# Gate and projection pieces ahead of the turns of probabilities on TensorE, in a decoder layer with two kinds of attention

## The chip, the core and the metric

The kernel runs on one core of one Trainium2 chip. The core has five engines that matter here, each working through its own instructions in order and waiting for the others by semaphores: TensorE (PE; matmuls, and transposes as matmuls with the identity), VectorE (DVE), ScalarE (ACT), GpSimd (POOL) and SyncE (SP, which issues the loads). The metric is the device time in microseconds; the figure for a kernel is the median of its runs.

## The reference

One layer of a decoder, 512 tokens of width 1024, all in 32-bit floats:

```
h = rms_norm(x)
q, k, v | q, kv of three branches | branch gates | merge gates = h @ w_in
y_A = block-sparse attention, 8 heads        y_B = three-branch attention, 8 heads, 2 kv groups
x = x + (sigmoid(gA) * (y_A @ W_A) + sigmoid(gB) * (y_B @ W_B)) @ w_o
x = x + (gelu(conv_a) * conv_b) @ w_down     conv = causal conv3 of rms_norm(x) @ w_up
x = x + sigmoid(x @ w_pg) * (p @ w_pp)
```

Queries and keys are normalised per head; a table of relative positions is added to every logit. With 512 tokens every block that attention may choose is chosen, so each branch is a causal softmax attention; the compressed branch has 31 keys.

## The kernel before, in words

A 32-bit product is made of three products of rounded operands: each factor is split into a high half (a copy rounded to the matmul's format) and a low half (the rest), and `three` (L1489) issues high x high, high x low and low x high. ScalarE or VectorE makes the high half, VectorE or GpSimd the low.

**Units.** The combined projection is cut into units w = 0 to 7, each a set of 256 to 384 columns (`ucols`). `project` (L1511) multiplies one unit with one tile tt of 128 tokens, in 8 pieces kt along the width of 1024; 3 matmuls make a piece. From unit 1 on a unit brings queries and keys for one pair of heads, n = w - 1 (unit 6: queries of two pairs). Its life: the weights are split (`w_high`, `w_low`, `split_unit`); TensorE projects; ScalarE copies the result out of its PSUM bank (`take_proj`, L838) and squares it; VectorE sums and makes a first guess of the root, GpSimd refines it in 12 small operations (`root`), VectorE normalises the tile (`normalise`, L1257); TensorE turns it (`turn_tile`, L1551) into PSUM bank 1; ScalarE and VectorE take high and low half out of it (`tile_high` L875, `tile_low` L1276). There is one such bank, so each tile waits for the low half of the one before.

**Gates.** The merge gates are 16 products of 128 columns by 512 tokens (`gate`, L1554), in 8 pieces kt of 3 matmuls, all into bank 7. ScalarE takes a gate by a tanh (`take_gate`, L918). For units 3 to 5 bank 7 is a projection bank too, for tiles 1 and 3 (`proj_bank`).

**Attention steps.** The work of attention is a list of 100 steps: 8 for each of the pairs 0 to 3, 17 for each of the pairs 4 to 7 (two branches, and one compressed step that ends the pair). A step t is one head's scores for one tile of queries, i + 1 blocks of 128 keys wide, i = 0 to 3 in turn. Each engine runs a loop over t. On TensorE step t has, before the change: the scores of t; the turn of the probabilities of t - 3 (`turn_probs`, L1650: `LAG` is 3); if due, a product with the values (`values`, L1672, 5 steps late); then pieces of a gate or of a projection that the tables `GATE` and `PROJ` give to this step; then the turn of a normalised tile if the table `TURN` says so. In a pair's first step the scores come behind the projection pieces, since they may need them. On ScalarE (L988 to L1016) the order in a step is:

```
take_gate, take_proj + squares (of what ended in step t-1); take_probs(t-3); tile_high(TURN[t-1]);
exp(t); gate_high; gather_strip; w_high(SPLIT[t])
```

VectorE has `bias(t)` (adds the position table and finds the maximum), `invert(t-1)`, the sums, `tile_low(TURN[t-1])`, `w_low(SPLIT[t])`, `normalise(TILE[t])` and the guess. GpSimd has `scale(t-1)`, its part of the splits, and `root`. The tables are filled by rules of step numbers (L119 to L150); no planner with costs is in it. Four banks of PSUM hold scores and turned probabilities, two each, so that step t's instructions wait for those of t - 2.

Of the kernel before, what the change touches and what calls it, by code (L numbers as in the profile page):

```python
# [73 lines left out]
def layer(nc, A, out):  # L74
    STEPS = attention_steps()
# [20 lines left out]
    GATE, j = {}, 2  # L96
# [24 lines left out]
    for w in range(2, W_UNITS):  # L121
        b0 = first_t[w - 2]
        if w == 2:
            start, counts, row = b0, (4, 4), ROWS - KT
        elif w < 6:
            start, counts, row = b0 - 4, (5, 6, 5, 5, 6, 5), 0
        elif w == 6:
            start, counts, row = b0 - 4, (4,) * 8, 0
        else:
            start, counts, row = b0 - 6, (2,) * 16, 0  # L130
        for a, count in enumerate(counts):
            PROJ[start + a] = (w, row, row + count)
            row += count
        split0 = b0 - 8 if w == 7 else b0 - 7
        for a in range(KT // 2):
            SPLIT[split0 + a] = (w, range(2 * a, 2 * a + 2))
        VALUES[start + len(counts)] = w
        ends = [t for t in sorted(PROJ) if PROJ[t][0] == w for r in range(*PROJ[t][1:]) if r % KT == KT - 1]
        for half in range(2):
            t = ends[2 * half + 1] + 1 if w > 2 else b0 + 2 * half  # L140
            GUESS[t] = (w, half)
            late = 1 if half and w < 6 else 0
            if late:
                ROOT[t + 1], ROOT[t + 2] = (w, half, range(1)), (w, half, range(1, 3))
            else:
                ROOT[t + 1] = (w, half, range(3))
            if w >= 6:
                late += 1
            for a in range(2):
                TILE[t + 2 + late + 2 * a], TURN[t + 3 + late + 2 * a] = (w, 2 * half + a), (w, 2 * half + a)  # L150

    def segments(t):

# [13 lines left out]
    LAG = 3  # L167
    VLAG = LAG + 2
# [43 lines left out]
    with ExitStack() as ctx:  # L212
# [123 lines left out]
        qkv_done = sem("qkv_done")  # L336
# [62 lines left out]
        def proj_bank(w, tt):  # L399

            if w == 0:
                return (0, 1, 4, 5)[tt]
            if w in (3, 4, 5):
                return 7 * (tt % 2)
            return 6 if w <= 2 and tt % 2 and (w, tt) != (2, 3) else 0

        def column(w, x):
# [1080 lines left out]
        def _(pe):  # L1488
# [22 lines left out]
            def project(w, tt, kts=range(KT)):  # L1511

                c = ucols(w)
                if kts[0] == 0:
                    before = 4 * w + tt - (1 if w > 5 or (w, tt) in ((2, 3), (3, 0)) else 2)
                    if before >= 0:
                        pe.wait_ge(qkv_done, before + 1)
                    if w in (3, 4, 5) and tt == 1:
                        pe.wait_ge(gate_tanh, w)
                for kt in kts:  # L1520
                    wait_weights(pe, w, kt)
                    pe.wait_ge(hT_lo, kt + 1)
                    t_ = slice(P * tt, P * (tt + 1))
                    ins = three(PS[:, proj_bank(w, tt), 0:c], hTh[:, kt, t_], hTl[:, kt, t_], Wh[:, kt, 0:c], Wl[:, kt, 0:c], kt == 0, kt == KT - 1)
                    if tt == NT - 1 and kt < KT - 1:
                        ins.then_inc(w_used, 1)
                if kts[-1] == KT - 1:
                    ins.then_inc(proj_filled, 1)
# [25 lines left out]
            def gate(j, kts=range(KT)):  # L1554

                if kts[0] == 0:
                    pe.wait_ge(g_lo[0], j + 1)
                    if j:
                        pe.wait_ge(gate_tanh, j)
                    if j == 2:  # L1560
                        pe.wait_ge(vc_done, 1)
                    if j in (3, 4, 5):
                        pe.wait_ge(qkv_done, 4 * j + 4)
                for kt in kts:
                    if kt == 4:
                        pe.wait_ge(g_lo[1], j + 1)
                    ins = three(PS[:, 7, :], Gh[j % 2][:, kt, :], Gl[j % 2][:, kt, :], hTh[:, kt, :], hTl[:, kt, :], kt == 0, kt == KT - 1)
                if kts[-1] == KT - 1:
                    ins.then_inc(gate_filled, 1)
# [152 lines left out]
            for t in range(T):  # L1722
                if STEPS[t]["k"]:
                    scores(t)
                if t >= LAG:
                    turn_probs(t - LAG)
                if t >= VLAG and STEPS[t - VLAG]["due"]:
                    values(t - VLAG)
                opens = t in PROJ and PROJ[t][1] % KT == 0
                if t in GATE and opens:  # L1730
                    gate(*GATE[t])
                if t in PROJ:
                    for part in segments(t):
                        project(*part)
                if not STEPS[t]["k"]:
                    scores(t)
                if t in GATE and not opens:
                    gate(*GATE[t])
                if t in TURN:
                    turn_tile(*TURN[t])  # L1740

# [186 lines left out]
```

## Time and profile before

| | |
|---|---|
| median of 3 runs | 888.48 us (887.63 to 891.33) |
| the profiled execution | 890.37 us, span 888.5 us |
| TensorE busy | 863.6 us, 97% |
| VectorE, ScalarE, GpSimd busy | 378.0, 405.8, 425.3 us (43, 46, 48%) |
| chain that ended last | 88% on TensorE |
| attention steps on TensorE | from about 82 to 372 us of the span |

A row of the timeline gives start, length, engine, line, operation, operands, the count of instructions merged in it and, in brackets, how long the engine had been idle before and who ended that. TensorE's matmuls are pipelined: the start of the next instruction, not the row's length, tells what one costs. Steps are found in the timeline by the scores: those of step 18 start at 151.63 us, those of step 30 at 197.65 us, those of step 38 at 220.01 us, those of step 93 at 351.01 us.

### The profile page before, as it was taken

To read this page: it belongs to the slowest core of one execution; us is meant where nothing else is said; L and a number is where in the kernel's file an instruction comes from. 1 tells how busy PE (TensorE), PEld (TensorE's weight loads), DVE (VectorE), ACT (ScalarE), POOL (GpSimd) and SP (SyncE) were. 2 spreads that over 40 slices of the span, in tenths; PEclk is the share of its full clock that TensorE was granted. 3 is DMA by queue.
4 is the path that set the end of the run, shared out by engine and by line. 5 is a ranking of instruction groups with operands and counts; after the bars stand their busy time and mean duration, and the time that the engine had idled before them with its cause. 6 is when DMAs were issued, how large, how long until landed. Compare 5 with 4: busy or idle time off the path is not lost.

```text
span 888.5 us, 13023 instructions
## 1 busy us (share of the span) xinstructions
PE 863.6 (97%) x4471; PEld 726.9 (82%) x4471; DVE 378.0 (43%) x864; ACT 405.8 (46%) x882; POOL 425.3 (48%) x547
## 2 busy tenths in 40 slices
PE   8999999999799999999999999999999999999998
PEld 8899889887688776788887888888888888888886
DVE  5446665555545534444417444444444440020223
ACT  5224656566646667533433744444444442231321
POOL 3841764554534345644552644444444444454440
PEclk9999999999999999999999999999999999999999
DMA  6944443342121226266531633333333333332214
GB/s 188 232 109 131 107 103 95 96 113 60 37 60 50 70 85 214 81 233 211 187 95 56 206 94 95 95 98 101 99 97 106 99 98 98 97 102 86 83 62 140
DMA packets 101363, 99.30 MB, mean 112 GB/s; under 512 B 15956, under 2 KB 76084, under 8 KB 101300
## 3 DMA queue, kind: packets, MB, share of 16 engines
q1 hardware_dynamic: 101247, 98.48, 37.7%
q8 instruction: 37, 0.61, 0.3%
q14 instruction: 26, 0.21, 0.1%
q10 hardware_dynamic: 53, 0.01, 0.0%
HBM read 87.58 MB, written 10.88 MB: 111 GB/s over the span
## 4 chain that ended last, share of the span: by engine, by line
PE 88%; DVE 4%; ACT 3%; issue 2%; POOL 2%; SPq 0%; DMA 0%; ACTq 0%; DVEq 0%; POOLq 0%
PE banks L1491 26%; PE banks L1492 25%; PE banks L1493 25%; PE banks L1672 3%; PE banks L1650 2%; PE banks L1630 1%; PE banks L1629 1%; PE banks L1551 1%; PE banks L1680 1%; ACT attention_split L875 1%; DVE plain_arena L1290 1%; DMA plain_arena<-in_conv_w_dram 0%; DVE plain_arena L1257 0%; PE banks L1579 0%; PE banks L1508 0%
## 5 line engine op out<-in xcount | busy, mean ns | idle before, releaser
L698 POOL TENSOR_TENSOR split_arena<-plain_arena,split_arena 128x512 fp32r<-128x512 f32 x184 | 240.2, 1318 | 252.0 <-ACT split_arena L932 232.5
L1491 PE MATMUL banks<-split_arena 128*128 128x512 f32 (+3 forms) x808 | 304.2, 376 | 5.3 <-ACT plain_arena L838 2.1
L1493 PE MATMUL banks<-split_arena 128*128 128x512 f32 (+3 forms) x808 | 296.8, 367 | 0.0
L1492 PE MATMUL banks<-split_arena 128*128 128x512 f32 (+3 forms) x808 | 296.7, 367 | 0.0
L932 ACT ACTIVATE split_arena<-plain_arena 128x512 fp32r<-128x512 f32 x184 | 112.9, 627 | 190.0 <-PE banks L1493 175.2
L1491 PEld LDWEIGHTS banks<-split_arena 128*128 128x128 f32 x808 | 152.4, 189 | 31.9 <-issue 3.5
L1493 PEld LDWEIGHTS banks<-split_arena 128*128 128x128 f32 x808 | 152.0, 188 | 21.1
L1492 PEld LDWEIGHTS banks<-split_arena 128*128 128x128 f32 x808 | 152.4, 189 | 20.3 <-issue 0.5
L1491 PE MATMUL banks<-late_arena,split_arena 128*128 128x512 f32 x240 | 93.8, 391 | 0.0
L1493 PE MATMUL banks<-late_arena,split_arena 128*128 128x512 f32 x240 | 93.5, 390 | 0.0
L1492 PE MATMUL banks<-late_arena,split_arena 128*128 128x512 f32 x240 | 93.5, 389 | 0.0
L1449 DVE SCALAR_TENSOR_TENSOR plain_arena<-banks,plain_arena 128x511 f32<-128x511 f32 x44 | 32.7, 743 | 133.2 <-ACT plain_arena L1041 133.2
L1290 DVE CUSTOM_DVE_ANT_0 plain_arena<-banks,plain_arena 128x128 f32<-128x128 f32 (+1 forms) x96 | 46.8, 487 | 74.0 <-PE banks L1630 73.8
L886 ACT ACTIVATE plain_arena<-plain_arena 128x128 f32<-128x128 f32 (+1 forms) x96 | 53.9, 562 | 37.7 <-DVE plain_arena L1290 37.5
L713 POOL TENSOR_SCALAR plain_arena<-plain_arena 128x128 f32<-128x128 f32 (+1 forms) x64 | 40.0, 627 | 61.3 <-DVE plain_arena L1308 61.1
L911 ACT ACTIVATE attention_plain<-banks 128x128 f32<-128x128 f32 (+1 forms) x96 | 41.3, 430 | 57.9 <-PE banks L1650 57.4
L1493 PEld LDWEIGHTS banks<-late_arena,split_arena 128*128 128x128 f32 x240 | 45.1, 188 | 9.5
L1491 PEld LDWEIGHTS banks<-late_arena,split_arena 128*128 128x128 f32 x240 | 45.1, 188 | 9.2
L1492 PEld LDWEIGHTS banks<-late_arena,split_arena 128*128 128x128 f32 x240 | 45.1, 188 | 9.2
L1650 PE MATMUL banks<-plain_arena 128*128 128x128 f32 x240 | 42.5, 277 | 1.7 <-POOL plain_arena L713 1.7
L1467 DVE TENSOR_TENSOR plain_arena<-banks,plain_arena 128x512 f32<-128x512 f32 x8 | 5.0, 683 | 86.5 <-PE banks L1493 86.5
L1041 ACT ACTIVATE plain_arena<-banks,plain_arena 128x512 f32<-128x512 f32 x44 | 30.6, 777 | 22.3 <-PE banks L1493 22.3
(193 smaller groups left out, 1113.4 us busy)
## 6 DMA issues: line engine op xcount, KB each, us to landing
plain_arena<-in_w_up_dram SPq DMA_DIRECT2D x88, 256.0 KB, 3.2
plain_arena<-in_w_down_dram SPq DMA_DIRECT2D x44, 256.0 KB, 2.6
plain_arena<-in_w_in_dram SPq DMA_DIRECT2D x18, 512.0 KB, 4.2
plain_arena<-in_w_in_dram SPq DMA_DIRECT2D x32, 192.0 KB, 4.0
plain_arena<-in_x_dram SPq DMA_DIRECT2D x8, 512.0 KB, 5.0
gates<-plain_arena SPq DMA_DIRECT2D x16, 256.0 KB, 2.4
plain_arena<-skew SPq DMA_DIRECT2D x16, 256.0 KB, 4.6
plain_arena<-gates SPq DMA_DIRECT2D x16, 256.0 KB, 3.6
```

Source lines behind the costliest of these rows:

```text
L698: pool.tensor_tensor(W2l[:, c % RING, :], raw2[:, c % RING, :], W2h[:, c % RING, :].bitcast(F32), ALU.subtract).then_inc(w2_lo, 1)
L713: pool.tensor_scalar(p_, p_, r, gsig[:, s["i"], h:h + 1], ALU.mult, ALU.mult).then_inc(scaled, 1)
L886: nc.scalar.activation(prob[:, t % 4, 0:nk], prob[:, t % 4, 0:nk], ACT.Exp, bias=mneg[:, t % 4:t % 4 + 1], scale=-1.0, accum_out=rsum[:, t ...
L911: nc.scalar.activation(PT[:, u % 4, 0:i + 1, P * i:P * (i + 1)], PS[:, 4 + t % 2, 0:P * (i + 1)].rearrange("p (j q) -> p j q", j=i + 1), A ...
L932: nc.scalar.activation(W2h[:, c % RING, :], raw2[:, c % RING, :], ACT.Copy).then_inc(w2_hi, 1)
L1041: nc.scalar.activation(dst[:, f % 2, :], PS[:, b, :], ACT.Identity, scale=cst[:, CONVW + 88 + col:CONVW + 89 + col], bias=cst[:, CONVB + c ...
L1290: nc.vector.tensor_tensor_reduce(out=prob[:, t % 4, 0:nk], in0=PS[:, 2 + t % 2, 0:nk], in1=strip[:, n % 2, e, S - nk:S], scale=1.0, scalar ...
L1449: link(nc.vector.scalar_tensor_tensor(out=dst[:, f % 2, 1:S], in0=PS[:, b, 0:S - 1], scalar=cst[:, CONVW + 44 + col:CONVW + 45 + col], in1 ...
L1491: nc.tensor.matmul(o, ah, bh, start=first, stop=False)
L1492: nc.tensor.matmul(o, ah, bl, start=False, stop=False)
L1493: return nc.tensor.matmul(o, al, bh, start=False, stop=last)
L1650: ins = nc.tensor.transpose(PS[:, 4 + t % 2, P * j:P * (j + 1)], prob[:, t % 4, P * j:P * (j + 1)], ident)
```

## The change

On TensorE, `turn_probs` and `values` move behind the gate and projection pieces of their step. Three tables change with it: the weights of unit 3 are split one step earlier (`split0`); the tiles of unit 6 are normalised three steps apart in place of two and turned two steps after; those of unit 7 are turned two steps after they are normalised. Unit 6 gets bank 7 for its tile 1, and the waits for projection banks are set accordingly.

```
-        split0 = b0 - 8 if w == 7 else b0 - 7
+        split0 = b0 - 8 if w in (3, 7) else b0 - 7
...
+            gap, lead = (3 if w == 6 else 2), (2 if w >= 6 else 1)
             for a in range(2):
-                TILE[t + 2 + late + 2 * a], TURN[t + 3 + late + 2 * a] = (w, 2 * half + a), (w, 2 * half + a)
+                TILE[t + 2 + late + gap * a], TURN[t + 2 + late + gap * a + lead] = (w, 2 * half + a), (w, 2 * half + a)
...
+            if w == 6:
+                return 7 * (tt == 1)
...
-                    before = 4 * w + tt - (1 if w > 5 or (w, tt) in ((2, 3), (3, 0)) else 2)
+                    before = 4 * w + tt - (1 if w > 6 or (w, tt) in ((2, 3), (3, 0), (6, 0), (6, 3)) else 2)
...
-                    if w in (3, 4, 5) and tt == 1:
+                    if w in (3, 4, 5, 6) and tt == 1:
...
+                    if j == 6:
+                        pe.wait_ge(qkv_done, 4 * 6 + 2)
...
                 if STEPS[t]["k"]:
                     scores(t)
-                if t >= LAG:
-                    turn_probs(t - LAG)
-                if t >= VLAG and STEPS[t - VLAG]["due"]:
-                    values(t - VLAG)
                 opens = t in PROJ and PROJ[t][1] % KT == 0
...
                 if t in GATE and not opens:
                     gate(*GATE[t])
+                if t >= LAG:
+                    turn_probs(t - LAG)
+                if t >= VLAG and STEPS[t - VLAG]["due"]:
+                    values(t - VLAG)
                 if t in TURN:
                     turn_tile(*TURN[t])
```

TensorE at the border of steps 17 and 18, before: the last matmuls of the projection of unit 4 (128x384), the scores of step 18, the turn of the probabilities of step 15 (4 blocks), and the first matmuls of gate 4 (128x512).

```order
L1491 MATMUL banks<-split_arena 128x384
L1492 MATMUL banks<-split_arena 128x384
L1493 MATMUL banks<-split_arena 128x384
L1629 MATMUL banks<-attention_split 128x384
L1630 MATMUL banks<-attention_split 128x384
L1650 MATMUL banks<-plain_arena 128x128 x4
L1491 MATMUL banks<-split_arena 128x512
L1492 MATMUL banks<-split_arena 128x512
```

The same place with the change; the lines have moved by 3 to 5 (L1655 is the turn, L1634 and L1635 the scores).

```order
L1494 MATMUL banks<-split_arena 128x384
L1495 MATMUL banks<-split_arena 128x384
L1496 MATMUL banks<-split_arena 128x384
L1655 MATMUL banks<-plain_arena 128x128 x3
L1634 MATMUL banks<-attention_split 128x384
L1635 MATMUL banks<-attention_split 128x384
L1494 MATMUL banks<-split_arena 128x512
L1495 MATMUL banks<-split_arena 128x512
```

The turn of step 14 (3 blocks), which stood ahead of the projection, now follows it, and the gate follows the scores of step 18 at once. ScalarE around the same border has the same operations in both: copy of the probabilities of step 14, two copies of a tile, the exponential, two weight conversions, and the projection tile's copy, on which the gate depends.

```order
L914 ACTIVATE attention_plain<-banks 128x3x128
L878 ACTIVATE attention_split<-banks,plain_arena 128x2x128 x2
L889 ACTIVATE plain_arena<-plain_arena 128x256
L846 ACTIVATE split_arena<-plain_arena 128x384 x2
L841 ACTIVATE plain_arena<-banks 128x384
```

These are rows with the change; before they read L911, L875, L886, L843 and L838 in the same order. Only the moment at which the first can start has moved.

TensorE in steps 40 and 41, before: scores (128x128), turn of 2 blocks, tile 2 of unit 6 (L1551), scores (128x256), turn of 3 blocks, gate 7.

```order
L1629 MATMUL banks<-attention_split 128x128
L1630 MATMUL banks<-attention_split 128x128
L1650 MATMUL banks<-plain_arena 128x128 x2
L1551 MATMUL banks<-plain_arena 128x128 x4
L1629 MATMUL banks<-attention_split 128x256
L1630 MATMUL banks<-attention_split 128x256
L1650 MATMUL banks<-plain_arena 128x128 x3
L1491 MATMUL banks<-split_arena,attention_split 128x512
```

The same steps with the change (L1554 is the turn of a tile).

```order
L1634 MATMUL banks<-attention_split 128x128
L1635 MATMUL banks<-attention_split 128x128
L1655 MATMUL banks<-plain_arena 128x128 x2
L1554 MATMUL banks<-plain_arena 128x128 x4
L1634 MATMUL banks<-attention_split 128x256
L1635 MATMUL banks<-attention_split 128x256
L1494 MATMUL banks<-split_arena,attention_split 128x512
L1495 MATMUL banks<-split_arena,attention_split 128x512
L1496 MATMUL banks<-split_arena,attention_split 128x512
L1655 MATMUL banks<-plain_arena 128x128 x3
L1554 MATMUL banks<-plain_arena 128x128 x4
```

Tile 1 is turned in step 40 now and tile 2 in step 41, right behind the turn of the probabilities of step 38.

## Rows read from the trace of the kernel before

**Rows 1.** The page: TensorE's busy share, and its granted clock in 40 slices.

```profile
PE 863.6 (97%) x4471; PEld 726.9 (82%) x4471; DVE 378.0 (43%) x864; ACT 405.8 (46%) x882; POOL 425.3 (48%) x547
...
PEclk9999999999999999999999999999999999999999
```

**Rows 2.** Waits of TensorE, 88 to 380 us: in total, times, longest.

```profile
PE banks L1551 <- DVE plain_arena L1257: 5.6, 4, 2.6
PE banks L1491 <- ACT plain_arena L838: 2.6, 3, 1.3
PE banks L1491 <- DVE split_arena L1173: 1.9, 2, 1.2
PE banks L1650 <- POOL plain_arena L713: 1.7, 3, 0.9
PE banks L1647 <- DVE plain_arena L1316: 1.3, 2, 0.8
```

**Rows 3.** Timeline of TensorE, two of these waits: start, length, operation.

```profile
204.21 0.39 PE L1491 MATMUL banks<-split_arena 128*128 128x256 f32 x1 [1.25 <-ACT plain_arena L838]
...
233.00 0.63 PE L1551 MATMUL banks<-plain_arena 128*128 128x128 f32 x4 [2.58 <-DVE plain_arena L1257]
```

**Rows 4.** Timeline of ScalarE in steps 17 and 18.

```profile
149.76 0.47 ACT L911 ACTIVATE attention_plain<-banks 128x384 f32<-128x384 f32 x1
150.13 0.83 ACT L875 ACTIVATE attention_split<-banks,plain_arena 128x256 fp32r<-128x256 f32 x2
150.84 0.52 ACT L886 ACTIVATE plain_arena<-plain_arena 128x256 f32<-128x256 f32 x1
...
151.33 0.94 ACT L843 ACTIVATE split_arena<-plain_arena 128x384 fp32r<-128x384 f32 x2
152.16 0.49 ACT L838 ACTIVATE plain_arena<-banks 128x384 f32<-128x384 f32 x1
```

**Rows 5.** Timeline of TensorE in the same steps.

```profile
148.69 0.49 PE L1650 MATMUL banks<-plain_arena 128*128 128x128 f32 x3
...
151.63 0.33 PE L1629 MATMUL banks<-attention_split 128*128 128x384 f32 x1
...
151.98 0.60 PE L1650 MATMUL banks<-plain_arena 128*128 128x128 f32 x4
152.80 0.47 PE L1491 MATMUL banks<-split_arena 128*128 128x512 f32 x1 [0.22 <-ACT plain_arena L838]
```

**Rows 6.** Timeline, steps 29 and 30: from a turn of probabilities to a normalised tile.

```profile
195.89 0.49 PE L1650 MATMUL banks<-plain_arena 128*128 128x128 f32 x3
...
196.42 0.49 ACT L911 ACTIVATE attention_plain<-banks 128x384 f32<-128x384 f32 x1 [3.50 <-PE banks L1650]
...
198.00 0.60 PE L1650 MATMUL banks<-plain_arena 128*128 128x128 f32 x4
...
198.85 0.68 DVE L1257 TENSOR_TENSOR plain_arena<-plain_arena 128x512 f32<-128x512 f32 x1
```

**Rows 7.** Timeline, step 37: from a turn of probabilities to a tile's low half.

```profile
218.98 0.49 PE L1650 MATMUL banks<-plain_arena 128*128 128x128 f32 x3
...
220.76 0.89 DVE L1276 SCALAR_TENSOR_TENSOR attention_split<-banks,plain_arena,attention_split 64x256 fp32r<-64x256 f32 x2 [1.07 <-ACT attention_split L875]
```

**Rows 8.** Timeline of ScalarE in steps 92 and 93.

```profile
349.82 0.49 ACT L911 ACTIVATE attention_plain<-banks 128x384 f32<-128x384 f32 x1 [0.43 <-PE banks L1650]
...
351.22 0.59 ACT L918 ACTIVATE plain_arena<-banks 128x512 f32<-128x512 f32 x1
```

**Rows 9.** Timeline of TensorE at the end of the attention steps.

```profile
362.05 0.27 PE L1650 MATMUL banks<-plain_arena 128*128 128x128 f32 x1
...
365.78 0.50 PE L1491 MATMUL banks<-split_arena 128*128 128x512 f32 x1 [0.66 <-POOL split_arena L771]
```

**Rows 10.** Stretches: length, busy time and count by engine, granted clock, DMA share, GB/s.

```profile
200.00:230.00 30.00, 26.37 (x182) 22.41 (x181) 17.78 (x64) 19.98 (x59) 14.97 (x37) 1.00 0.18 54
...
233.00:237.00 4.00, 4.00 (x14) 3.41 (x15) 2.67 (x9) 3.51 (x11) 2.20 (x3) 0.57 0.21 63
```

## The prediction

> **What bounds the kernel now.** I read the page first: TensorE is busy 97% of the span and its granted clock is 9 tenths or more in every slice [rows 1]. So the order of its work can bring no more than its waits, and it can cost whatever new waits it makes. The second view is the list of TensorE's waits over 88 to 380 us, the stretch with the attention steps [rows 2]. Five kinds matter: turning a normalised tile waits for VectorE's normalisation (5.6 us in 4), a gate or projection waits for ScalarE to empty a projection bank (2.6 in 3), a projection waits for split weights (1.9 in 2), a turn of probabilities waits for GpSimd's scaling (1.7 in 3) or, after a compressed step, for VectorE (1.3 in 2). Together 13.1 us: the most that a better order can win in waits. The third view is the timeline of all engines at single steps, to see what stands in front of the releaser on its own engine.
>
> **What the change moves.** The matmuls stay the same in number and size. In each step TensorE turned the probabilities of three steps before right after the scores; now it does so after the gate and projection pieces. ScalarE's order hardly changes. In its step t it empties a finished projection bank, squares it, copies the turned probabilities of t-3, copies the high half of a tile turned in step t-1, does the exponentials of t, and converts weights. It is in order, so everything behind the copy of probabilities now begins only when TensorE is through with the step's long pieces.
>
> **What goes.** (a) The split of unit 3 comes a step earlier: 1.9 us go. (b) Unit 6 alternates its banks and its tiles are turned a step later, so the wait at 204.21 (1.25 us) and the four tile waits (5.6) go, in the form in which they stand here [rows 2, 3]. (c) The turns after a compressed step get a gate piece as cover: 1.3 go. Of the 1.7 behind GpSimd the two small ones go (0.8); the largest, 0.9, sits behind twelve root operations that start later too, and I keep it. With the rest of the 2.6 (two gate waits, 1.4, counted again below at their new size) that is 12.2 us gone.
>
> **What comes, first term: the gates of pairs 1 to 3.** Step 18 is the pattern. Gate 4 shares bank 7 with projection tile 3 of unit 4, which ends in step 17. Before, TensorE turned the probabilities of step 14 at 148.69, ahead of that projection [rows 5]; ScalarE copied them at 149.76, then did the tile (150.13), the exponential (150.84) and two weight conversions (151.33), and took the projection at 152.16 [rows 4]. That is 2.40 us of ScalarE work, all of it under the projection; the gate began at 152.80, 0.22 us late [rows 5]. Now the turn comes after the projection. From the start of a turn of three blocks to its copy are 0.53 us when ScalarE is free (195.89 to 196.42 [rows 6]); then the same 2.40, the bank copy 0.49 and 0.15 to the gate's start: 3.57. TensorE has between them only the turn and the next scores, 0.34 + 0.35 = 0.69 (151.63 to 151.98 is such a score; the turn is 0.25 to the next start, and 0.09 longer for what follows it). So it waits 3.57 - 0.69 = 2.9 us. Step 10 is the same; in step 26 the weights are 256 wide and the wait is 2.7. Sum 8.5 us. Bounds: 0 if ScalarE's work were still covered, 8.5 as worked out; nothing that I see covers it, since TensorE and ScalarE both run in order, and I take 8.5.
>
> **Second term: tiles of unit 5 and the last tile of unit 6.** From a turn of probabilities to the end of the normalisation of the next tile but one are 3.64 us (195.89 to 198.85 + 0.68 [rows 6]), because bank 1 and VectorE's queue hold it behind the previous tile. This chain starts at the end of step 29 now. TensorE has the turn, the scores and twelve narrow matmuls, 2.11 us (195.89 to 198.00 [rows 6]), and another turn of four, 0.44, then wants the tile: 1.1 us late, and in step 32, by a shorter chain in a shorter step, the same. Tile 3 of unit 6 waits for tile 2's bank in step 34 by the sum of the first term: 2.8 less 1.45 of cover, 1.3. Sum 3.5 us; bounds 0 and 3.5; I take 3.5.
>
> **Third term: tiles 1 and 2 of unit 6.** The new table turns them in steps 40 and 41, one behind the other. Tile 2 needs bank 1, so VectorE's low half of tile 1, which follows ScalarE's high half, which stands behind the copy of the probabilities of step 38; and these are turned immediately before tile 2. From turn to end of low half are 2.67 us (218.98 to 220.76 + 0.89 [rows 7]); with 0.34 for the turn itself and 0.1 to start, TensorE waits 2.4 us. This wait is structural. I take it in full.
>
> **Smaller ones.** At the start of step 95 gate 15 waits for ScalarE to take gate 14. Before, a value product of 2.4 us stood ahead of the gate and covered that. Now the gate goes first: from the turn at the end of step 92, 0.53 + 1.99 (349.82 to 351.22 + 0.59 [rows 8]) + 0.15 = 2.7 against 1.9 of cover (three turns and three scores, estimated from the lengths in [rows 5, 6]): 0.8. The like at steps 66, 78 and 83, and the scores of step 69, make 1.3. Weight pieces of units 4, 5 and 7, converted behind the late copy, come 0.7, 0.7 and 1.1 late; two bank waits of unit 7 add 0.9, gate 7 and the tile at step 40 add 1.7. Sum 7.2 us. Each rests on three or four durations in a row, and a TensorE held up earlier gives the others time; bounds 0 and 7.2, I take half, 3.6. At the end of the attention ScalarE's last exponential (turn at 362.05 [rows 9]) moves back by a gate piece of 1.45 us, and with it the copies that release GpSimd's low half (L771), for which the matmul at 365.78 waits: 1.0 us, bounds 0 and 1.5.
>
> **The clock.** In 233 to 237 us the granted clock is 0.57 on average, that is 1.2 GHz for most of it, right behind the 2.58 us wait at 233.00 [rows 3, 10]; 4.0 x 0.43 = 1.7 us of full-speed work are lost. In 200 to 230 us, with the wait of 1.25 us at 204.21, it was 2.4 GHz throughout. The new waits of 2.9, 2.9, 2.7 and 2.4 lie at the size that cost a fall once. I take two falls against the one here: +1.7 us; bounds -1.7 (none) and +5.1 (four). The Trainium skill, "TensorE: Matmul & The Clock Gate", section "Why this matters for your kernels", says that idle gaps between bursts of matmuls bring the clock back to half. [...]
>
> **The sum.** -12.2 + 8.5 + 3.5 + 2.4 + 3.6 + 1.0 = +6.8, and 1.7 for the clock: +8.5 us. The profiled execution took 890.37 us (span 888.5), 1.9 above the median of 888.48; I put the difference on the median: 897.0 us. With all smaller waits and four falls it is 888.5 + 10.4 + 5.1 = 904.0. With only the first and third terms, no new fall and all that goes gone, it is 888.5 - 12.2 + 8.5 + 2.4 - 1.7 = 885.5.
>
> **Rivals.**
> Rival 1, faster: the projection banks are emptied in time. ScalarE idles under the projection now, and if it reached the bank copy within the 0.69 us that TensorE has, the first term would be nothing and the removed waits would be the result: with the third term, half of the second and no fall, 888.5 - 12.2 + 2.4 + 1.8 - 1.7 = 878.8. It decides from 0.69 us of ScalarE work behind the turn; rows 4 show 2.40. For it speaks that in steps with little work ScalarE is idle for 3 us and more (3.50 at 196.42 [rows 6]). 6%.
> Rival 2, no change: only the structural waits come, the others are taken up by slack that the earlier ones make; between the 885.5 above and one with half the second term and one fall, 889: 888. 18%.
> Rival 3, the clock decides: all four long waits drop it, and the smaller waits come in full: 904. Slower than the forecast, same sign. 20%.
> The forecast itself, new ScalarE waits larger than what goes, 892.5 to 901: 56%.
>
> **How the numbers follow.** A change of 0.5% is 4.4 us, about what a measurement of this kernel can tell from none. Faster by more is rival 1: 0.06. Within it is rival 2 with a little of the forecast's lower edge: 0.20. Slower: 0.74. The range leaves out rival 1, the lower half of rival 2 and the top of rival 3: 888 to 904; the forecast's own range is 892.5 to 901.
>
> **What would show it.** TensorE's list of waits should have a line of some 8.5 us in three for a gate's first matmul behind ScalarE's bank copy (L838 here), each near 2.9, at steps 10, 18 and 26. A tile turn behind VectorE's low half (L1276 here), near 2.4, should stand once, two scores after the one at step 40. The split-weight waits near 98 and 101 us should be gone, and the waits behind the compressed steps too. ScalarE should sit idle under each long projection and be busy behind it. The prediction fails if those three gate waits are under 1 us each, or if their sum is right and the time is still below 889: then slack elsewhere gave it back, and the list of waits will lack the rest of my terms. After each wait of over 2 us the granted clock of the next 4 us tells the last term.

## The result, and the profile after

The changed kernel takes **913.50 us** (median of 3 runs, 912.53 to 915.76) against 888.48: a ratio of 1.0281, 95% interval 1.0259 to 1.0303. It is 25 us slower. The direction was forecast, the size was not: the median lies 16.5 us above the 897.0 that I predicted and 9.5 us above the end of my range.

The profiled execution took 913.5 us, its span is 911.6, so 23.1 us more than the span before. The page after, to be held against [rows 1]:

```profile
PE 870.5 (95%) x4471; PEld 731.3 (80%) x4471; DVE 377.1 (41%) x864; ACT 404.7 (44%) x882; POOL 425.7 (47%) x547
...
PEclk9999999999999999999999999999999999999999
```

The counts of instructions are what they were, and VectorE, ScalarE and GpSimd are busy as long as before, within 1.1 us; TensorE is busy 6.9 us longer, most of it from a slower clock (below), while its share fell from 97 to 95%. The clock line hides what happened to the clock: each fall, a stretch of a few microseconds at 1.2 GHz, is much shorter than a slice. The largest of TensorE's waits after, 60 to 420 us, are these (total, times, longest). Over this stretch all of its waits sum to 30.4 us, and before to 15.3; the lines that answer are in [rows 2], which cover 88 to 380 us, with line numbers lower by 3 to 5.

```profile
PE banks L1494 <- ACT plain_arena L841: 11.0, 7, 2.7
PE banks L1554 <- DVE attention_split L1279: 5.6, 4, 2.4
PE banks L1554 <- DVE plain_arena L1260: 4.6, 4, 1.7
PE banks L1655 <- POOL plain_arena L716: 2.4, 1, 2.4
PE banks L1494 <- ACT plain_arena L921: 1.9, 3, 0.9
PE banks L1494 <- POOL split_arena L774: 1.5, 1, 1.5
```

The first line is what the first term is about. The second, a tile's turn behind VectorE's low half, does not stand in [rows 2] at all. The gate of step 18, on ScalarE and TensorE, answers to [rows 4, 5]:

```profile
157.39 0.49 PE L1655 MATMUL banks<-plain_arena 128*128 128x128 f32 x3
...
157.91 0.49 ACT L914 ACTIVATE attention_plain<-banks 128x384 f32<-128x384 f32 x1 [2.01 <-PE banks L1655]
158.30 0.83 ACT L878 ACTIVATE attention_split<-banks,plain_arena 128x256 fp32r<-128x256 f32 x2
159.01 0.52 ACT L889 ACTIVATE plain_arena<-plain_arena 128x256 f32<-128x256 f32 x1
...
159.50 0.94 ACT L846 ACTIVATE split_arena<-plain_arena 128x384 fp32r<-128x384 f32 x2
160.33 0.49 ACT L841 ACTIVATE plain_arena<-banks 128x384 f32<-128x384 f32 x1
...
160.96 0.47 PE L1494 MATMUL banks<-split_arena 128*128 128x512 f32 x1 [2.73 <-ACT plain_arena L841]
```

From the turn (157.39) to the gate (160.96) are 3.57 us, exactly the sum of the first term: ScalarE is idle for 2.01 us under the projection, then does in a row what it did under the projection before, and TensorE stands still for 2.73 us. The clock, in stretches of 4 us right behind five long waits (length, busy time and count by engine, granted clock, DMA share, GB/s), answers to [rows 10]:

```profile
126.10:130.00 3.90, 3.90 (x21) 3.33 (x22) 2.07 (x5) 0.73 (x2) 1.13 (x2) 1.00 0.93 221
...
161.00:165.00 4.00, 4.00 (x22) 3.43 (x23) 1.09 (x5) 0.86 (x3) 1.56 (x2) 1.00 0.26 66
...
195.60:199.60 4.00, 4.00 (x12) 3.15 (x13) 1.73 (x5) 0.30 (x1) 0.79 (x2) 0.63 0.42 86
...
247.10:251.10 4.00, 4.00 (x16) 3.43 (x17) 1.20 (x4) 1.15 (x3) 1.70 (x3) 0.60 0.50 131
...
309.80:313.80 4.00, 4.00 (x15) 3.38 (x16) 1.36 (x4) 1.21 (x4) 1.91 (x3) 0.63 0.00 0
```

The two longest waits (2.73 us at 126.07 and 160.96) left the clock at 2.4 GHz; those of 2.52, 2.32 and 2.41 us dropped it to 1.2 GHz for some 3.4 us, 1.7 us of work each, and so did one of 1.54 us at 387.96. Four falls against one before are three more: 5.1 us.

The account of the span: waits 15.1, clock 5.1, and 1.7 by which the attention steps began later in this execution. I don't count that start as an effect of the change: the first wait of the stretch, at 84.87 us here and 83.17 before, lies anywhere from 81.6 to 84.5 us in the profiled executions of the ten variants below. Together 21.9 of 23.1 us; 1.2 are not assigned.

### The profile page after: what moved, and what is told of

It reads as the page before. It is cut to its first block, busy times and chain, and to the rows that moved or that the text cites. A ratio compares the mean times of both kernels' runs of the same rounds, so it can differ in the third digit from the quotient of the medians.

```text
span 911.6 us, 13024 instructions
## 1 busy us (share of the span) xinstructions
PE 870.5 (95%) x4471; PEld 731.3 (80%) x4471; DVE 377.1 (41%) x864; ACT 404.7 (44%) x882; POOL 425.7 (47%) x547
## 4 chain that ended last, share of the span: by engine, by line
PE 85%; ACT 4%; DVE 4%; issue 3%; POOL 2%; DMA 1%; SPq 1%; ACTq 0%; DVEq 0%; POOLq 0%
PE banks L1494 25%; PE banks L1496 24%; PE banks L1495 24%; PE banks L1677 3%; PE banks L1655 2%; PE banks L1634 1%; ACT attention_split L878 1%; PE banks L1635 1%; PE banks L1554 1%; ACT plain_arena L889 1%; ACT split_arena L846 1%; POOL split_arena L686 1%; DVE attention_split L1279 1%; PE banks L1685 1%; DMA plain_arena<-in_conv_w_dram 1%
## 5 line engine op out<-in xcount | busy, mean ns | idle before, releaser
L686 POOL TENSOR_TENSOR split_arena<-plain_arena,split_arena 128x384 fp32r<-128x384 f32 (+1 forms) x28 | 31.2, 1117 | 42.2 <-ACT split_arena L846 32.2
L1655 PE MATMUL banks<-plain_arena 128*128 128x128 f32 x240 | 43.1, 279 | 2.5 <-POOL plain_arena L716 2.4
L1279 DVE SCALAR_TENSOR_TENSOR attention_split<-banks,plain_arena,attention_split 64x256 fp32r<-64x256 f32 (+2 forms) x56 | 24.1, 448 | 43.0 <-ACT attention_split L878 42.6
```

Of the source, the lines that this page charges most:

```text
L686: pool.tensor_tensor(Wl[:, kt, 0:c], raw[:, kt, 0:c], Wh[:, kt, 0:c].bitcast(F32), ALU.subtract).then_inc(w_lo[1], 1)
L1279: ins = nc.vector.scalar_tensor_tensor(out=dst, in0=PS[r0:P, 1, P * v0:P * v1].rearrange("p (v c) -> p v c", v=v1 - v0), scalar=cst[r0:P, ...
L1655: ins = nc.tensor.transpose(PS[:, 4 + t % 2, P * j:P * (j + 1)], prob[:, t % 4, P * j:P * (j + 1)], ident)
```

## Experiments

Ratios are against the kernel before on the same chip, in brackets the 95% interval.

**1. The move alone.** The kernel before with its own tables; only `turn_probs` and `values` stand behind the pieces, as in the change:

```
-                if t >= LAG:
-                    turn_probs(t - LAG)
-                if t >= VLAG and STEPS[t - VLAG]["due"]:
-                    values(t - VLAG)
...
                 if t in GATE and not opens:
                     gate(*GATE[t])
+                if t >= LAG:
+                    turn_probs(t - LAG)
+                if t >= VLAG and STEPS[t - VLAG]["due"]:
+                    values(t - VLAG)
```

> The kernel before with one part of the change alone: the turns of probabilities and the value products behind the gate and projection pieces; tables, banks and waits of before. Theory (the loss comes from the move, by way of ScalarE's in-order queue; the tables win back some of it): the three gate waits of 2.5 to 2.7 us and the tile waits for bank 1 are there, and the waits that the tables take away (splits, unit 6) are there too, so 916 to 926 us, slower than the whole change. Rival (the new tables, with tiles turned in neighbouring steps, are the loss): 888 to 896 us.

Measured 919.78 us, 1.0331 (1.0289 to 1.0372). The profiled execution, the slowest of four, has seven falls of the clock. Its largest waits in 60 to 420 us:

```profile
PE banks L1491 <- ACT plain_arena L838: 15.2, 9, 2.7
PE banks L1551 <- DVE plain_arena L1257: 10.2, 5, 2.6
PE banks L1491 <- DVE split_arena L1173: 3.8, 4, 1.9
PE banks L1551 <- DVE attention_split L1276: 2.4, 1, 2.4
```

The move alone makes the whole of the loss. With the tables beside it the time is 4.4 us less by the ratios (0.0050 x 888.5). The uncertainty of that difference is about 4 us by the two intervals, so it is likely, and no more, that the tables give back a part of the loss.

**2. The tables alone.** The changed kernel with the two calls back right behind the scores.

> The change without the move: probabilities are turned right after the scores, as before, with the new tables, banks and waits. Theory: the removed waits of before are pure gain: 1.9 (splits) + 1.3 (bank of unit 6) + some 5 of the tile waits + 1.7 for the fall of the clock behind the longest of them, 9.9 us, so 877 to 882 us. Rival (the tables are the loss): 900 us or more.

Measured 891.30 us, 1.0029 (1.0013 to 1.0045): the forecast of 877 to 882 was wrong. Its largest waits in 60 to 420 us:

```profile
PE banks L1554 <- DVE attention_split L1279: 4.6, 3, 2.6
PE banks L1655 <- POOL plain_arena L716: 3.9, 4, 2.5
PE banks L1554 <- DVE plain_arena L1260: 2.8, 3, 1.8
```

The waits of (a) and (b) are gone from their places; of (c) one of 0.8 us stays (at 336.52), since without the move no gate piece covers it. As many new ones stand there: all waits of the stretch sum to 15.3 us, as before. The large ones are at 95.38 (1.84 us, tile of step 3), at 108.17 (1.23 us), at 229.10 (tile 2 of unit 6, step 41) and at 289.30 (2.46 us, a turn behind GpSimd's scaling). The mean granted clock of the ten executions is 0.995 in the median, against 0.998 for the kernel before on the same chip; that is 2.7 us, as much as the time measured. Steps 40 and 41 show the pattern (timeline):

```profile
225.92 1.05 ACT L926 ACTIVATE split_arena<-plain_arena 128x1024 fp32r<-128x1024 f32 x1
...
226.87 0.48 ACT L914 ACTIVATE attention_plain<-banks 128x384 f32<-128x384 f32 x1
227.24 0.84 ACT L878 ACTIVATE attention_split<-banks,plain_arena 128x256 fp32r<-128x256 f32 x2
...
228.15 0.90 DVE L1279 SCALAR_TENSOR_TENSOR attention_split<-banks,plain_arena,attention_split 64x256 fp32r<-64x256 f32 x2
...
229.10 1.12 PE L1554 MATMUL banks<-plain_arena 128*128 128x128 f32 x4 [2.56 <-DVE attention_split L1279]
```

It is the wait of my third term, without the move (2.56 us here, with the clock at 0.50 in the 4 us behind it): two tiles turned one step apart through one bank. What holds ScalarE up in front of the halves is another thing here, a gate's conversion of 1.05 us (L926) where the changed kernel has the late turn. So the neighbouring turns of the tables are enough for this wait, and the move is not needed for it.

**3. Probabilities early in the three gate steps.** The changed kernel; only in steps 9, 17 and 25 the turn stands ahead of the projection again.

```
+                early = t in (9, 17, 25)
+                if early:
+                    turn_probs(t - LAG)
                 opens = t in PROJ and PROJ[t][1] % KT == 0
...
-                if t >= LAG:
+                if t >= LAG and not early:
                     turn_probs(t - LAG)
```

> The changed kernel, but in steps 9, 17 and 25 alone (the projection that ends a unit's last tile, ahead of a gate in the same bank) the probabilities are turned before the projection, as in before. Theory: the three gate waits (2.73, 2.73, 2.52 us) fall to the size of before (1.2 and 0.2 and none), -6.6 us, and one fall of the clock less, -1.7: 904 to 908 us. Rival (a shorter wait here comes back at the next tile or bank wait): 910 us or more, with the tile waits longer by as much.

Measured 904.81 us, 1.0185 (1.0157 to 1.0213): 8.5 us less by the ratios (0.0096 x 888.5). The line of bank copies falls from 11.0 to 5.6 us; the gates of steps 10, 18 and 26 still wait, 1.56, 0.62 and 0.40 us. So 5.4 of the first term's 8.0 us of waits are shown to hang on the turn ahead of the projection; 6.6 were expected. The other 3.1 us of the 8.5 are no more than the uncertainty of the difference (about 3 us by the two intervals). The rival is out: all other waits of TensorE behind 100 us and up to 400 us are the same as in the changed kernel, to within 0.05 us. One fall of the clock fewer was expected as well; the profile has four again, two of them at other waits than in the changed kernel.

**4. ScalarE's copy last in its step.** The changed kernel with TensorE's order untouched.

```
-                if LAG <= t:
-                    take_probs(t - LAG)
                 if t - 1 in TURN:
                     tile_high(*TURN[t - 1])
...
                 if t in EARLY:
                     split_chunk(EARLY[t])
+                if LAG <= t:
+                    take_probs(t - LAG)
```

> The changed kernel with ScalarE's order in a step altered: the copy of the turned probabilities comes last, behind the tile's high half, the exponential and the weight conversions. TensorE's order is that of the change. Theory (ScalarE's copy of probabilities holds up all that stands behind it): the gate waits fall from 2.7 to about 1 us each, the tile waits for VectorE's low half (5.6 us) to under 1, and two or three falls of the clock go: 892 to 900 us. Rival (TensorE's own order is at fault, through the later scaling and values): 909 us or more.

Measured 884.43 us, 0.9949 (0.9937 to 0.9962): 29 us less than the changed kernel and 4.5 less than the one before, 8 us under the range that I expected. In 60 to 420 us the waits sum to 14.3 us in place of 30.4 (the three gates 1.62, 0.71 and 0.70; tiles behind the low half 3.5 in place of 5.6, where I expected under 1), the profile has no fall of the clock there in place of four (6.8 us), and the attention steps begin 3.0 us earlier, at 81.86. These make 25.9 of the 29.1 us between the two spans; 3.2 are not assigned. The same step as above, in this kernel:

```profile
149.75 0.82 ACT L878 ACTIVATE attention_split<-banks,plain_arena 128x256 fp32r<-128x256 f32 x2
150.47 0.51 ACT L889 ACTIVATE plain_arena<-plain_arena 128x256 f32<-128x256 f32 x1
150.96 0.93 ACT L846 ACTIVATE split_arena<-plain_arena 128x384 fp32r<-128x384 f32 x2
151.79 0.48 ACT L914 ACTIVATE attention_plain<-banks 128x384 f32<-128x384 f32 x1
152.16 0.49 ACT L841 ACTIVATE plain_arena<-banks 128x384 f32<-128x384 f32 x1
```

Halves, exponential and conversions lie under the projection; only the copy and the bank copy follow the turn (151.24), and the gate waits 0.71 us (152.79) in place of 2.73. This shows the cause: with the turn as late as in the changed kernel, the loss is gone once ScalarE, which works in order, no longer holds the rest of the step behind the copy of that turn.

**5. Tile 2 of unit 6 a step later.**

```
+                apart = 1 if (w, half, a) == (6, 1, 0) else 0
-                TILE[t + 2 + late + gap * a], TURN[t + 2 + late + gap * a + lead] = (w, 2 * half + a), (w, 2 * half + a)
+                TILE[t + 2 + late + gap * a], TURN[t + 2 + late + gap * a + lead + apart] = (w, 2 * half + a), (w, 2 * half + a)
```

> The changed kernel with one entry of the table other: tile 2 of unit 6 is turned in step 42, not in 41, so that a step lies between it and tile 1. Theory (TensorE waits for bank 1 because the two turns are neighbours and ScalarE's high half stands behind the late copy of probabilities): the wait of 2.3 us goes, and with it the fall of the clock that began 0.8 us into the next matmuls, 1.7 us: 909 to 911.5 us. Rival (the wait moves to the next tile or scores): 913 us or more.

Measured 908.71 us, 1.0226 (1.0202 to 1.0249), 4.9 us less. The wait at tile 2 shrinks from 2.32 to 0.84 us; I had expected it to go.

```profile
245.43 0.66 PE L1555 MATMUL banks<-plain_arena 128*128 128x128 f32 x4 [0.84 <-DVE attention_split L1280]
```

That is 1.5 us. The profile has one fall of the clock in place of four, but it is the fastest of four executions (906.66 us, mean granted clock 0.998; the others 0.992, 0.991 and 0.989, the changed kernel 0.990, 0.990 and 0.984). By the medians the clock gives 1.4 us. The other 2 us lie within the uncertainty of the difference (about 3 us).

**6. Idle time filled with matmuls.** The changed kernel with 10, 8 and 8 extra matmuls, whose results nobody reads, in the waits of steps 26, 41 and 63. They can't shorten what TensorE waits for; they only keep it at work.

```
+            def fill(t, count):
+
+                pe.wait_ge(biased, t)
+                for _ in range(count):
+                    nc.tensor.matmul(PS[:, 3 - t % 2, :], hTh[:, 0, 0:P], hTh[:, 0, :], start=True, stop=True)
...
+                if t == 26:
+                    fill(t, 10)
...
+                if t == 63:
+                    fill(t, 8)
...
+                if t == 41:
+                    fill(t, 8)
```

> The changed kernel with matmuls that compute nothing put into three of its long waits, in a bank of scores that is free there: 10 ahead of gate 5 in step 26, 8 ahead of the tile in step 41, 8 ahead of the turn of probabilities in step 63 (each 0.23 us; the waits there are 2.5, 2.3 and 2.4 us). The waits last as long as before. Theory (each fall of the clock behind such a wait costs 1.7 us of its own): two or three of the falls go and the time drops by 3.4 to 5.1 us, 908.5 to 910.5 us. Rival (the falls are bookkeeping, or hidden behind other waits): 913 us or more, by what the filler overhangs.

Measured 908.06 us, 1.0223 (1.0202 to 1.0243): 5.2 us less than the changed kernel by the ratios, with 26 matmuls more. From the scores of step 26 to the gate are 3.12 us in both kernels (192.47 to 195.59 in the changed one, 193.69 to 196.81 here), so the work on the way to the gate is as long as it was. Behind it the clock is now full, where it was at 0.63:

```profile
196.80:200.80 4.00, 3.98 (x22) 3.39 (x23) 1.75 (x5) 0.82 (x3) 0.81 (x2) 1.00 0.47 86
```

In 306 to 314 us it is full too; two falls stand in this profile at other places (161.7 and 243.6). The second of them lies over step 41: its eight extra matmuls take 3.21 us, where the eight of step 63 take 1.98, and they overhang the wait. From the start of gate 7 to tile 2 are 4.54 us (243.09 to 247.63) in place of 3.57. The profile is the slowest of the four executions. Over all of them the mean granted clock is 0.9955 in the median against 0.990: 5.0 us less lost to the clock, which is the 5.2 us measured and the price of three falls. The uncertainty of the 5.2 is about 3 us.

**7. ScalarE copies a step later.** The aim is that of experiment 4, but the copies of t - 4 come right behind `take_proj`, so that none of them waits for TensorE in its own step; ScalarE's loop makes one pass more.

```
-                if LAG <= t:
-                    take_probs(t - LAG)
+                if LAG < t:
+                    take_probs(t - LAG - 1)
```

> The changed kernel with ScalarE's copy of turned probabilities a step later in its program: in step t, right after the projection's copy, it copies those of t-4, which TensorE turned at the end of step t-1; then tile, exponential and weights as before. Theory: nothing on ScalarE waits for the end of TensorE's step any more; the gate waits fall from 2.7 to some 0.2 us (with the copy last in its step they kept 0.7 to 1.6), so 880 to 884 us. Rival (with the copy so late, TensorE waits for the banks of turned probabilities or the value products): 888 us or more.

Measured 883.78 us, 0.9946 (0.9925 to 0.9967), not to be told from experiment 4 (0.9949). Its largest waits in 60 to 420 us:

```profile
PE banks L1494 <- ACT plain_arena L841: 2.8, 4, 1.3
PE banks L1554 <- DVE attention_split L1279: 2.3, 2, 1.5
```

11.0 us of bank waits have become 2.8 (the gates of steps 10 and 18 wait 1.28 and 0.33 us, that of step 26 not at all), and a new kind appears, turns that wait for the bank which the late copy holds (1.7 us in two). That is the wait of the rival, too small here to decide the time.

**8. Experiments 7 and 5 together.**

> The lagged copy of probabilities and the tile of step 41 moved to 42 together. Theory: beside the lagged copy alone, the tile wait of 1.5 us that was left at step 41 goes too: 1 to 2 us under it, 879 to 883 us. Rival: with the queue of ScalarE in order the place of that tile costs nothing more, and both are within 0.5 us of each other.

Measured 882.78 us, 0.9931 (0.9911 to 0.9952), the lowest median of all, though 7 and 8 can't be told apart. The tile wait of 1.52 us (at 227.08 in experiment 7) is gone, and one of 0.67 us for split weights stands 6 us further on.

**9. Control: ScalarE's order in the kernel before.** The edit of experiment 4 on the kernel before.

> The kernel before, with TensorE's order and tables untouched; only ScalarE's copy of the turned probabilities stands last in its step, as in the run that won with the move. Theory (ScalarE's order pays only because the move puts the turn behind the long pieces, where the copy blocks tile halves, the exponential, conversions and the bank copy): here the turn comes right behind the scores, ScalarE gets it early, and the copy last delays only the value products, which have two steps of slack: 888 to 892 us, ratio 1.000 to 1.004, and TensorE's waits for the bank copy (L838) stay at 2 to 3 us in sum. Rival (the copy's place was a fault of the kernel before by itself, and the move's win is due to that alone): 882 to 886 us, as with both.

Measured 890.05 us, 1.0010 (0.9998 to 1.0023). Its largest wait in 60 to 420 us:

```profile
PE banks L1650 <- ACT attention_plain L911: 5.2, 7, 1.7
```

These are turns that wait for the late copy, 5.2 us that the kernel before does not have. In return the tile waits behind VectorE's normalisation fall from 5.6 to 1.5 us. The copy's place brings nothing in sum where the turn comes early, but by an exchange of waits and not, as I had expected, because nothing hangs on it. That the late turn is what makes the late copy pay is not shown by itself: experiment 4 has the new tables too, and the tables with the late copy but without the move were not run.

**10. The split of unit 3 back.** The kernel of experiment 8 with the first line of the change undone.

```
-        split0 = b0 - 8 if w in (3, 7) else b0 - 7
+        split0 = b0 - 8 if w == 7 else b0 - 7
```

> The changed kernel with ScalarE's copies of probabilities one step later and tile 2 of unit 6 turned one step later (0.9931 of the kernel before), now with the weights of unit 3 split at their old step. Theory (the earlier split puts a low half on GpSimd, which itself waits 1.00 us for its high half and takes 1.02 us, ahead of the 12 root operations of tile 2 of unit 2, and so causes the 1.7 us wait of a tile turn in step 3): that wait goes, the two waits for split weights near 98 and 101 us (1.9 us) come back, and the time is the same within 1 us: 882 to 884 us, ratio 0.993 to 0.995. Rival (the wait in step 3 belongs to the moved turn): it stays, the split waits come back too: 884.5 to 886 us.

Measured 883.97 us, 0.9940 (0.9922 to 0.9957). Waits in 88 to 104 us, first of experiment 8, then of this one:

```profile
PE banks L1555 <- DVE plain_arena L1261: 1.7, 1, 1.7
```

```profile
PE banks L1495 <- DVE split_arena L1177: 2.2, 2, 1.3
```

One is exchanged for the other. GpSimd shows why (timeline of the changed kernel):

```profile
92.34 1.02 POOL L686 TENSOR_TENSOR split_arena<-plain_arena,split_arena 128x384 fp32r<-128x384 f32 x1 [1.00 <-ACT split_arena L846]
93.32 0.20 POOL L726 TENSOR_TENSOR plain_arena<-plain_arena 128x8 f32<-128x8 f32 x1
...
97.03 0.69 DVE L1260 TENSOR_TENSOR plain_arena<-plain_arena 128x512 f32<-128x512 f32 x1 [2.34 <-POOL plain_arena L732]
...
97.87 0.63 PE L1554 MATMUL banks<-plain_arena 128*128 128x128 f32 x4 [1.72 <-DVE plain_arena L1260]
```

The earlier split stands ahead of the 12 root operations on GpSimd, waits 1.00 us for its high half and takes 1.02; the tile that needs the root comes 1.72 us late.

## Why the prediction was right in direction and wrong in size

**The step that failed: three sizes in the sum.** The mechanism of the loss, ScalarE held up by the late turn, was forecast and is there. The sum put nothing on waits at four places that then measured 6.3 us; it halved the smaller waits (3.6 taken, 6.9 measured); and it took two falls of the clock where the profile has four (1.7 taken, 5.1 measured). The first is the largest.

**What goes (12.2 us): right on its face, wrong as a gain.** The waits that I listed in (a), (b) and (c) are gone. But I priced the tables by the waits they remove and looked for new ones mainly behind the move. Experiment 2 measured the tables by themselves: +0.3%, with as much waiting as before, where I expected 7 to 12 us less. Of the new waits there my sum had only the third term. For (a), "1.9 us go" had a price of 1.72 us on another engine (experiment 10).

**First term (8.5 us): right.** 2.73 + 2.73 + 2.52 = 8.0 us, predicted 2.9, 2.9, 2.7. Each is some 0.2 under what I worked out. Experiment 4 shows the cause (1.62, 0.71 and 0.70 us left), experiment 3 most of the size. Rival 1, which needed ScalarE at the bank copy in 0.69 us, is out: the first long work behind the turn is still the 2.40 us of [rows 4]. But its mechanism is what experiment 4 builds, and the time is then 884, where the rival had 878.8.

**Second term (3.5 us): right.** 1.09 (215.32), 1.24 (221.03) and 1.17 (226.58): 3.5 us.

**Third term (2.4 us): right in size**, 2.32 at 247.08. The table makes it without the move (experiment 2). The old table with the move is no better there: the tiles of unit 6 then wait 1.58, 2.42 and 2.64 us (experiment 1).

**Smaller ones: worked out rightly, then halved on a weak ground.** At the places that I named and right beside them are 6.9 us of waits (split weights 0.48, 0.47 and 0.68; gate 7 and its tile 0.92 and 0.55; seven others of 0.20 to 0.90, 3.8 in all), against 7.2 worked out and 3.6 taken. The ground for halving, that a TensorE held up earlier gives the others time, did not hold: in experiment 3 the gates wait 5.4 us less, and the later waits are the same to within 0.05 us, so they do not depend on how long TensorE was held up before. That fits with ScalarE's work hanging on TensorE's turn, which each wait moves back as well. That is 3.3 us of the miss.

**End of the attention (1.0 us): right**, 1.54 us (at 387.96) in place of the 0.66 of [rows 9]: +0.9.

**Missed: 6.3 us.** The tile of step 3 (1.72); the second tile of unit 2 at 111.94 (2.44); the turn of step 63 behind GpSimd's scaling (2.41, where I had kept 0.9); and 0.58 at 211.06. The second and the last stand in experiment 1 too (2.44 and 0.58), so the move makes them; the other two come with the tables. The second is the chain of the first and third terms at a place where I had not drawn it, from the turn through copy and halves to the freed bank:

```profile
108.90 0.60 PE L1655 MATMUL banks<-plain_arena 128*128 128x128 f32 x4
109.54 0.60 ACT L914 ACTIVATE attention_plain<-banks 128x512 f32<-128x512 f32 x1 [1.09 <-PE banks L1655]
110.03 0.83 ACT L878 ACTIVATE attention_split<-banks,plain_arena 128x256 fp32r<-128x256 f32 x2
...
110.89 0.99 DVE L1279 SCALAR_TENSOR_TENSOR attention_split<-banks,plain_arena,attention_split 64x256 fp32r<-64x256 f32 x2 [1.30 <-ACT attention_split L878]
...
111.94 0.66 PE L1554 MATMUL banks<-plain_arena 128*128 128x128 f32 x4 [2.44 <-DVE attention_split L1279]
```

The third stands in experiment 2 too (2.46), so it comes with the tables. GpSimd's row is the same in the kernel before: a scaling of 128x384, 12 root operations, and the scaling that TensorE waits for. What is new is that a tile of unit 7, turned a step later, has its low half on VectorE (first row, experiment 2) ahead of the reciprocal that the first of these scalings waits for. So GpSimd begins that one 0.81 us later (second row, experiment 2; third row, before), and all that follows it too, while TensorE comes to these steps 0.76 us earlier (a score of 128x384 at 286.50 in place of 287.26). That makes the 1.57 us from 0.89 to 2.46.

```profile
281.60 1.12 DVE L1279 SCALAR_TENSOR_TENSOR attention_split<-banks,plain_arena,attention_split 64x256 fp32r<-64x256 f32 x3 [0.95 <-ACT attention_split L878]
284.03 0.66 POOL L716 TENSOR_SCALAR plain_arena<-plain_arena 128x384 f32<-128x384 f32 x1 [2.92 <-DVE plain_arena L1311]
...
283.22 0.66 POOL L713 TENSOR_SCALAR plain_arena<-plain_arena 128x384 f32<-128x384 f32 x1 [1.05 <-DVE plain_arena L1308]
```

**The clock (+1.7 us, bounds to +5.1): at the bound.** Four falls, as rival 3 had it, but not at the places it named: two of its four waits left the clock alone, and two places that it did not know had one. That is 3.4 us of the miss. That there are just four in this profile is partly chance: which waits bring a fall differs between executions (last section). Rival 3, with the smaller waits in full, was the right account of what I had seen; it lacked the 6.3 us that I had not, and so its 904 was still 9.5 low.

The miss in the sum of waits is 15.1 - 6.8 = 8.3 us: smaller ones +3.3, missed +6.3, the terms that came out slightly short -0.7 (0.5, 0.1 and 0.1), which leaves -0.6; of it -0.4 is an idle time of TensorE at 405.32 in the kernel before that the changed one does not have, the rest is rounding. With 3.4 for the clock it is 11.7. The rest up to 16.5 is the start (1.7), the 1.2 not assigned, and 1.9 by which the profiled execution before lay above its median while that after did not (11.7 + 1.7 + 1.2 + 1.9 = 16.5, to the rounding).

What I can't settle: why one wait drops the clock and a longer one does not. Experiment 6 shows only that filling the waits keeps the clock up behind them (1.00 behind the fillings of steps 26 and 63, in place of 0.63 and 0.63).

## What to carry to other kernels

When an operation is moved later on one engine, write down for every engine that consumes it what stands behind the consumer in its queue: in an in-order queue the whole rest of the step moves with it. The cure follows from the same list: move the consumer behind the work that does not need it (29 us here, experiment 4). A table that removes a wait is not priced until the instructions it moves are followed on the other engines as well, and a sum of small waits, each worked out, is kept whole.

## What was not expected of the hardware

The length of a wait alone does not decide whether the granted clock falls. In the changed kernel's profile 2.73 us (twice) and 2.44 us did not bring it down; 2.52, 2.41, 2.32 and 1.54 us did, each for about 3.4 us at 1.2 GHz. And the same wait goes both ways from one execution to another. Behind the gate of step 18 (2.73 to 2.74 us) the clock over the next 4 us is 1.00 in the changed kernel and in experiment 5, and 0.63 and 0.64 in experiments 1 and 6. Behind the wait of 1.53 to 1.54 us at the end of the attention it is 0.57 to 0.59 in the changed kernel and in experiments 1 and 3, and 1.00 in experiments 5 and 6. Short waits can be followed by a fall too: 0.57 behind 1.34 us (experiment 9, at 225.49), 0.59 behind 1.35 us (experiment 7, at 358.31), and 0.57 behind 0.92 us (experiment 6, at 243.09). The variant of experiment 4 has a wait of 1.62 us at 120.67 with the clock at 1.00 in the 4 us behind.

The Trainium skill, "TensorE: Matmul & The Clock Gate", section "Why this matters for your kernels", warns of idle gaps between bursts of matmuls, but of longer ones than any of these. So it does not put the four waits of the prediction in danger, and by it the sum there would have had no new fall. The traces differ from it: behind gaps of 1.3 to 2.6 us the clock did fall, though not each time, and the measurement decides. So compare kernels by the mean granted clock of all their executions, and not by the falls in one profile.
